# Where the transfers of the weight sums run, and where the second half's input and its sums are made

## What is computed

```python
def conv_ffn(x, prev, w_gate, w_up, w_dw, w_down):
    g = x @ w_gate
    g_ext = jnp.concatenate([prev.astype(g.dtype), g], axis=1)
    g_c = depthwise_causal_conv(g_ext, w_dw)
    y = (jax.nn.gelu(g_c, approximate=True) * (x @ w_up)) @ w_down
    return y, g_ext[:, -(FFN_CONV_WIDTH - 1):]

def trunk(x, conv_prev, ffn_prev, past_k, past_v, p):
    for layer in range(DEPTH):
        hn = rms_norm(h, p['norm_mix_pre'][layer])
        ...                                  # conformer_conv_module, or K/V, Q and attention
        h = h + rms_norm(m, p['norm_mix_post'][layer])
        f, st_f = conv_ffn(rms_norm(h, p['norm_ffn_pre'][layer]), ffn_prev[layer], ...)
        h = h + rms_norm(f, p['norm_ffn_post'][layer])
```

## Time and profile before

| | us |
|---|---|
| runs | 3136.15, 3144.06, 3147.18 |
| median | 3144.06 |
| profiled execution | 3141.24 |
| its span | 3139.5 |
| PE busy | 3004.6 (96%) |
| DVE busy | 1922.6 (61%) |
| ACT busy | 1431.9 (46%) |
| POOL busy | 518.0 (16%) |
| DMA: q1 and q0, share of 16 engines | 55.0% and 16.9% |

### The profile page before, as it was taken

How to read it: one execution, slowest core, us unless ns; L and a number is a source line. 1 busy time by engine, 2 the same in 40 slices (tenths; PEclk the granted TensorE clock), 3 DMA queues, 4 the chain that set the end, 5 groups by cost and what they waited for, 6 DMA issues and landing times.

```text
span 3139.5 us, 62628 instructions
## 1 busy us (share of the span) xinstructions
PE 3004.6 (96%) x24274; PEld 2598.1 (83%) x24274; DVE 1922.6 (61%) x2846; ACT 1431.9 (46%) x2709; POOL 518.0 (16%) x738
## 2 busy tenths in 40 slices
PE   8999999899799999999999999999999899899999
PEld 7987887678799998998777777777887677799998
DVE  6998676544677445634666666666476653577532
ACT  5445632223355333323676777777443223255422
POOL 0211000010100101221333333333000010200100
PEclk9999999999899999999999999999999999999999
...
GB/s 128 84 71 88 81 277 275 280 216 192 188 297 244 167 106 165 177 169 198 347 387 403 395 403 399 403 398 380 176 152 306 271 279 189 166 281 269 223 109 85
DMA packets 560090, 739.67 MB, mean 236 GB/s; under 512 B 29186, under 2 KB 407419, under 8 KB 559721
## 3 DMA queue, kind: packets, MB, share of 16 engines
q1 hardware_dynamic: 511318, 589.87, 55.0%
q0 software_dynamic: 48384, 145.60, 16.9%
...
## 4 chain that ended last, share of the span: by engine, by line
PE 68%; DVE 12%; DMA 12%; ACT 3%; issue 3%; SPq 0%; DVEq 0%; ACTq 0%
PE PS L1186 31%; PE PS L1638 11%; DMA raw<-in_ffn_w_up 7%; PE PS L2746 7%; PE PS L2782 4%; PE PS L2758 4%; DVE mT L989 4%; DVE wlo L417 3%; PE PS L2801 2%; DMA raw<-in_ffn_w_down 2%; PE PS L2820 2%; PE PS L2811 2%; ACT whi L412 2%; DMA weight_parts_kept<-wlo 1%; DVE cv L1899 1%
## 5 line engine op out<-in xcount | busy, mean ns | idle before, releaser
L417 DVE TENSOR_TENSOR wlo<-raw,whi 128x1024 fp32r<-128x1024 f32 (+1 forms) x300 | 359.5, 1198 | 698.6 <-ACT whi L412 690.8
L412 ACT CAST whi<-raw 128x1024 fp32r<-128x1024 f32 (+1 forms) x298 | 306.2, 1027 | 892.0 <-PE PS L1186 427.5
L1186 PE MATMUL PS<-xfh,whi 128*128 128x512 f32 (+3 forms) x1152 | 405.6, 375 | 80.1 <-DVE wlo L417 76.6
L1186 PE MATMUL PS<-xfh,wlo 128*128 128x512 f32 (+3 forms) x1152 | 398.4, 369 | 0.0
L1186 PE MATMUL PS<-xfl,whi 128*128 128x512 f32 (+3 forms) x1152 | 398.0, 368 | 0.0
L1186 PEld LDWEIGHTS PS<-xfh,whi 128*128 128x128 f32 x1152 | 213.7, 194 | 126.4 <-issue 91.7
L2746 PE MATMUL PS<-ident,kr 128*128 128x128 f32 x2048 | 277.2, 276 | 2.6 <-ACT kt L2916 2.6
L2746 PEld LDWEIGHTS PS<-ident,kr 128*128 128x128 f32 x2048 | 224.8, 141 | 39.0 <-issue 37.2
L3009 DVE COPY kt<-PS 128x512 f32<-128x512 f32 x256 | 172.6, 681 | 130.2 <-PE PS L2746 128.1
L1186 PEld LDWEIGHTS PS<-xfh,wlo 128*128 128x128 f32 x1152 | 212.5, 193 | 34.2
L1186 PEld LDWEIGHTS PS<-xfl,whi 128*128 128x128 f32 x1152 | 213.3, 194 | 32.8 <-issue 0.5
...
## 6 DMA issues: line engine op xcount, KB each, us to landing
kr<-in_cache_k SPq DMA_DIRECT2D x256, 512.0 KB, 7.5
vr<-in_cache_v SPq DMA_DIRECT2D x256, 512.0 KB, 7.2
...
weight_sums<-in_ffn_w_up POOLq DMA_DIRECT2D x24, 1088.0 KB, 10.9
weight_sums<-in_ffn_w_gate POOLq DMA_DIRECT2D x24, 1088.0 KB, 9.1
```

Of the source, the lines that this page charges most:

```text
L412: nc.scalar.copy(whi[b][:, 0:blocks_of(t), :], raw[t % RAWS][:, 0:blocks_of(t), :]).then_inc(w_hi, 1)
L417: nc.vector.tensor_tensor(wlo[t % RAWS][:, 0:n, :], raw[t % RAWS][:, 0:n, :], whi[b][:, 0:n, :].bitcast(F32), ALU.subtract).then_inc(w_lo, 1)
L1186: mm = nc.tensor.matmul(PS[:, s + c, 0:c1 - c0], stationary(wt, t, kw + k), x(k0 + k)[:, c0:c1], start=start and k == 0 and wt is whi and ...
```

## The change

- **Weight sums elsewhere.** Layer 0: 12 in glu (two after the shifts of each of six blocks), 8 in out00 and out01 (one per two tiles), 7 in up00 (at every third f), 5 in down00. Layer 1: 16 in down01 (two after each output store), 16 in kv0 and kv1 (one at every second n), none in up10 and down10. They are counted by a semaphore of their own (`sums_made`), and the stored rows of the residual by `kept_out` alone.
- **Input of the second half in place.** `x32` is now the second half of `hT` itself, whose old content has been stored in DRAM. down00 and down10 write the scaled float32 input there, from which `xfh` and `xfl` are made (before, it was written to `xfl32`, the place of `xfl`, and so lost when `xfl` was made); the eight instructions at line 1988 are gone; DVE waits for the stored rows at i = 14 of down.
- **Input sums by DVE**, at the start of half 1 of up, in place of POOL. SP waits for them, because the first weight sums are loaded into `hT`. `t_hi` and `t_lo` are made in the order 0, 2, 1, 3, two at f = 0 and f = 1 (ACT), two at f = 1 and f = 2 (DVE), and PE waits for each where it is used.
- **Output of half 0 added one step later** (`post_part`: f = 4, 6, ... instead of 2, 4, ...).

```diff
-    x32 = slots("x32", [P, KB, NH], F32, 32)
+    x32 = hT[:, :, AT0[1]:AT0[1] + NH]
@@ glu_pool
                 shifts(pool, m + 1, 1)
                 buffer_free(m)
+                weight_sum(pool, 0, 2 * m)
+                weight_sum(pool, 0, 2 * m + 1)
             last_shifts(pool, 0, 1)
...
+            for i in range(KB):
+                pool.wait_ge(w_used, first["out00"] + 2 * i + 3)
+                weight_sum(pool, 0, 12 + i)
@@ paired_sp
             if g == 0:
-                sp.wait_ge(kept_out, kept_count(layer, SUMS, KB))
+                sp.wait_ge(sums_made, 16 * SUMS * (layer + 1))
+                sp.wait_ge(kept_out, rows_kept(layer))
+                sp.wait_ge(sx_t, SX_T + 4 * (layer + 1))
@@ paired_pe
+            def sums_ready(n):
+                if g == 0:
+                    pe.wait_ge(sx_l, SX_L + 4 * layer + n)
+
+            sums_ready(1)
             if g == 0:
-                pe.wait_ge(sx_l, SX_L + 4 * (layer + 1))
@@ up_act
-                if half == 1 and f == 1:
-                    act.wait_ge(sx_t, SX_T + 4 * (layer + 1))
-                    for n in range(4):
+                if half == 1 and f <= 1:
+                    for n in SUM_ORDER[2 * f:2 * f + 2]:
+                        act.wait_ge(sx_t, SX_T + 4 * layer + n + 1)
                         nc.scalar.copy(t_hi[:, n], t32[:, n]).then_inc(sx_h, 1)
@@ up_dve
+            def input_sums():
+                b11, b12 = x32[:, 0:HK, 0:HC], x32[:, 0:HK, HC:NH]
+                b21, b22 = x32[:, HK:KB, 0:HC], x32[:, HK:KB, HC:NH]
+                dve.wait_ge(w_used, t0 + 2)
+                nc.vector.tensor_tensor(t32[:, 0], b12, b11, ALU.subtract).then_inc(sx_t, 1)
+                nc.vector.tensor_tensor(t32[:, 1], b12, b22, ALU.subtract).then_inc(sx_t, 1)
+                dve.wait_ge(sx_t, SX_T + 4 * layer + 1)
+                nc.vector.tensor_tensor(t32[:, 2], t32[:, 0], b22, ALU.subtract).then_inc(sx_t, 1)
+                dve.wait_ge(sx_t, SX_T + 4 * layer + 3)
+                nc.vector.tensor_tensor(t32[:, 3], b21, t32[:, 2], ALU.add).then_inc(sx_t, 1)
@@ post_part
-                if f >= 2 and f % 2 == 0 and f // 2 - 1 < KB:
-                    k = f // 2 - 1
+                if f >= 4 and f % 2 == 0 and f // 2 - 2 < KB:
+                    k = f // 2 - 2
@@ up_dve, half 1
-                dve.wait_ge(w_used, t0 + 2)
-                for k in range(KB):
-                    nc.vector.scalar_tensor_tensor(out=x32[:, k, :], in0=hT[:, k, tokens(1)], scalar=...,
-                                                   in1=rs_x[:], op0=ALU.mult, op1=ALU.mult).then_inc(sx_x, 1)
+                input_sums()
...
-                if half == 1 and f == 1:
-                    for n_ in range(4):
-                        dve.wait_ge(sx_h, SX_H + 4 * layer + n_ + 1)
+                if half == 1 and 1 <= f < FS0:
+                    for i in range(2 * f - 2, 2 * f):
+                        dve.wait_ge(sx_h, SX_H + 4 * layer + i + 1)
+                        n_ = SUM_ORDER[i]
@@ down_act and down_dve
+            lo32 = x32 if half == 0 else lo32
@@ down_dve
+                if half == 0 and i == 14:
+                    dve.wait_ge(kept_out, rows_kept(layer))
@@ down_pool
-                    if half == 0:
-                        for i in range(FB, SUMS):
-                            if (i - FB) * KB // (SUMS - FB) == n:
-                                weight_sum(pool, layer, i)
+                    if half == 0 and layer == 0 and n < 5:
+                        weight_sum(pool, 0, 27 + n)
+                    if half == 1:
+                        weight_sum(pool, 1, 2 * n)
+                        weight_sum(pool, 1, 2 * n + 1)
@@ up_pool
                 for f in range(FB):
-                    pool.wait_ge(w_used, first[f"up{layer}0"] + 2 * f + 3)
-                    weight_sum(pool, layer, f)
+                    if layer == 0 and f % 3 == 2:
+                        pool.wait_ge(w_used, first["up00"] + 2 * f + 3)
+                        weight_sum(pool, 0, 20 + f // 3)
...
-                input_sums(pool, layer)
@@ kv_pool
+                if n % 2 == 0:
+                    weight_sum(pool, 1, 16 + KB * half + n // 2)
```

36 lines of the change are left out of this document (15 added, 21 removed).

## The result

The changed kernel takes 3103.9 us (median of four runs, 3100.8 to 3107.9), the kernel before 3141.4 us beside it (3136.2 to 3147.2). The ratio is 0.9881, with a 95% interval of 0.9858 to 0.9903: 37 us are gained, half of the 74 that were forecast. The profiled execution took 3104.8 us, with a span of 3103.1, which is 36.4 us less than the span of before.

The account below looks back on a forecast made before the run. TensorE, busy 96%, was taken to bound the kernel, losing time to late weight tiles as sums share the DMA engines. Savings of -96 and costs of +22 gave -74 on 3141.2: 3067 us, range 3035 to 3105.

Parts of the forecast that it names:

- the first: Adding sums stay slow everywhere, 11 to 12 us; first stage costs 13, K/V start 20: +17, 3084 us; chance 0.14.
- the second rival: First-half up stages bound by parts and raw tiles alone, giving 10 each instead of 24: +28, 3095 us; chance 0.09.
- What bounds the kernel, and the relief of the first-half stages: Late weight tiles hold TensorE; moving sums out saves 24 us in up00, 24 in up10, 5 in down00, 9 in down10.
- The start of half 1: Start of the second half: input kept in place and sums on VectorE save 18 us in layer 0, 16 in layer 1.
- Twelve sums in the first stage: Last shifts in glu queue behind two adding sums and land at about 258: +9 us, bounds +6 and +13.
- Sixteen sums in down01: GpSimd falls behind, delaying K/V loads and first K store: +7 us (+2 to +20); late raw tiles in down01: +2.
- Sixteen sums in the K/V stages: One sum per two tiles in kv0 and kv1, traffic staying below the up stages': +3 us (0 to +10).
- what would prove it wrong altogether: Sign against the forecast: K/V raw tiles landing in over 9 us, or TensorE waiting 10 us or more per up stage.
- The fourth: K/V stages become bound by the software queue, every tile pair waiting: +91 in place of +3, 3155 us; chance 0.04.
- The third: GpSimd's queue costs nothing because sums land fast in empty stages: -13, 3054 us; chance 0.10.
- the fifth: Up stages stay as long as before; only -34 from the second half's start remains, with +22: 3129 us; chance 0.03.

## Why the prediction was half right

The time lies 1 us inside the stated range of 3035 to 3105, and that is luck. The upper end was said to take in the first and the second rival, but their 17 and 28 us on 3067 make 3112, and the second rival had no part in what happened. The gains were sized well, term by term; the costs were 61.7 us where the sum had 22, and three of its steps failed.

*What bounds the kernel, and the relief of the first-half stages*: right. The four terms (up00, up10, down00, down10) had 24, 24, 5 and 9 us and came to 19.9, 27.3, 2.8 and 13.3. The count of 44 tiles at 5.50 us as the floor of an up stage holds to a microsecond. What it had not seen is that nearly all of the stages' loss lay with the adding sums: in the kernel before no wait of PE over 1 us stands ahead of the first of them, which is issued at 484.71 in up00 and at 2408.08 in up10. It had the landing times of a copy and of an adding sum, and left 5 us for the four adding ones of up00, which kept 10. The second rival (stages bound by parts and raw tiles) is refuted by up10's 241.6 us.

*The start of half 1*: right in size, 18 and 16 us forecast, 17.6 and 14.2 measured. (For layer 1 the working adds 10.4, 3 and 2 to 15.5, where they make 15.4, and no row shows the 3 and the 2.) It was argued from DVE's 11.39 against 1.73 us beside POOL's additions, and the run with POOL's additions put back shows it at work, though it takes back a third of the gain only: the additions begin 3.2 us into the stretch there (770.84) and are over when VectorE comes to its four steps. The Trainium skill ("SBUF — State Buffer", "Who interferes with whom") lets a VectorE operation with at most one SBUF input run beside GpSimd unless it is in a two-port mode, which it says copies can enter. What VectorE's mode was the trace doesn't show; the copy of two elements that took 5.74 us has one input and was held until POOL's third addition was over.

*Twelve sums in the first stage*, +9: the mechanism is right and the size is wrong. The step that failed is the landing time, "an adding sum lands in 8.7 us at the lightest load in the trace". The last shift lay at 265.9 instead of 258. Of these 7.9 us, 3.9 are the first sum's landing (12.6 us), 1.0 the second's (9.5 where 8.5 was reckoned), 2.2 that POOL came to them later than 238.6, and 0.8 the shift's own landing behind the sum. With the 8.8 us from 249.24 to 258 that had been reckoned this makes 16.7 on PE, and another 2.6 us were lost between there and up00, where the sum had 1. The run with the pair later gives 17.3 us back by moving the two. With copies in their place (8.0 and 9.2 us) the wait was still 11.17 us, so the place costs more than the kind here.

The Trainium skill ("DMA: Bandwidth & Descriptors", "Anatomy of one DMA") would put a transfer of this size at an estimated 4.6 us. No sum in the changed kernel's trace is that fast: its 32 copies take 5.4 to 8.2 us, its 32 adding ones 8.5 to 14.3.

*Sixteen sums in down01*, +7 and +2: measured 17.7 and 2.1. The step that failed is again the landing time, 8.7 to 8.8 us for the adding ones, which landed in 8.5 to 12.7, 10.2 on average over the eight. POOL fell behind further: the last sum was issued at 1209.24 and landed at 1218.4, and as down01 began 21.9 us earlier than in the kernel before, that is 1240 on its scale, where 1225 was reckoned. And what came first was overlooked: not the first K store at the third tile but the last output store at the first. The working counted three stores back from the last one, at 1203.56, and did not ask what that last store would itself stand behind: sum 13. The run with twelve in down01 and none in kv0 has the stage back at 96.2 us, so the loss belongs to the last four. That they cost by the queue's order and not by sharing the engines rests on the landing: the store, issued 0.6 us behind sum 13, lands 0.8 us after it.

*Sixteen sums in the K/V stages*, +3: measured 22.6 by the run without them. The step that failed compared GB/s ("below what the up stages move") and not what the engines are busy with. 230 and 243 GB/s filled 0.88 and 0.89 of the engines' time, while the kernel before moved 270 at 0.93. It is the adding bytes that are dear, at twice the engine time of copied ones. Raw tiles come by SP's hardware queue and were late all the same. The slowest of them, issued at 1331.9 in kv1 (KB, us from issue to landing; in kv0 the slowest took 11.8):

```profile
raw<-in_w_k SPq DMA_DIRECT2D x1, 512.0 KB, 12.9
```

In the kernel before none took over 6.2 us there. ACT stood up to 6.48 us in kv0 and 8.46 in kv1 for such tiles. This is sharing of the engines, not order in POOL's queue. The forecast had named raw tiles that land in over 9 us in the K/V stages as what would prove it wrong altogether; five of their 32 did. The share is no full measure either: with eight copies in up01, kv0 had a share of 0.92 and was only 4.1 us longer than without sums.

Of the rivals the first, that adding sums stay slow wherever they run, is the one that came nearest, and for its reason, though they landed in 10.7 us on average and not in 11 to 12. Its price of 17 us was still too small by 23, mostly because it let only the two ends of stages pay and not the K/V stages in between. The fourth had the right place and the wrong mechanism: had POOL's queue paced the pairs, the sixteen sums of the K/V stages would have cost 5.7 us each, where they cost 1.4. The third is refuted by the first stage, the fifth by the up stages; the second was answered above.
